# Expert stage of a two-layer hybrid decoder step: one unrolled stream over both expert tables instead of a u pass and a v pass per tile

## The chip, the cores and the metric

One core of one Trainium2 chip. The time is device microseconds (us) of the whole program, median of several runs. Everything is float32.

## What is computed

One inference step of a trunk of two layers (DEPTH = 2) for 512 prompt tokens and 8 decoding sequences. A layer has three token mixers, an output projection, and then the PEER feed-forward part, which the change is about. Cut to that part:

```python
def peer_ffn(h, wq, sub_keys, u_tab, v_tab):
    ...
    s = jnp.einsum('nhpk,hpek->nhpe', q, sub_keys).astype(jnp.float32)
    s1, i1 = lax.top_k(s[:, :, 0], PEER_TOPK)
    s2, i2 = lax.top_k(s[:, :, 1], PEER_TOPK)
    ...
    top_s, pick = lax.top_k(cand_s, PEER_TOPK)
    idx = jnp.take_along_axis(cand_i, pick, axis=-1).reshape(n, PEER_HEADS * PEER_TOPK)
    gate = jax.nn.softmax(top_s, axis=-1).reshape(n, PEER_HEADS * PEER_TOPK)
    ...
        act = jax.nn.gelu(jnp.einsum('nd,ned->ne', xk, u_tab[ik]).astype(jnp.float32), approximate=False)
        return jnp.einsum('ne,ned->nd', (gk * act).astype(v_tab.dtype), v_tab[ik])
```

Each token picks 8 heads x 16 = 128 experts of 16384. An expert is a row of 1024 floats in table u and one in table v. A token's output is the sum over its 128 experts of gate x gelu(u row . x) x v row.

## The kernel before

**Tiling.** The 512 prompt tokens are four tiles (t = 0 to 3) of 128 tokens, a token to a partition. One *gather* is an indirect DMA from POOL that fetches, for one of the 128 slots, one row of a table for each of the 128 tokens: 128 rows of 4 KB, 524,288 bytes, into one buffer of 128x1024. A tile needs 128 gathers from u and 128 from v; a layer 1024. The 8 decoding tokens are a fifth, small tile that comes behind them with 16 gathers (line 1614).

**Order.** The expert stage is one block in which the engines run programs of their own, tied by semaphores. POOL goes through the tiles, in each first through all of u, then all of v, in a loop over 16 slots (line 1602). For each four slots it waits for four free buffers of a ring of 16 (line 1604), copies four columns of indices to a small tile (line 1605), waits for this copy (line 1606) and issues four gathers (line 1608).

DVE takes the buffers in the same order. In the u half of a tile it multiplies a buffer by the token's activations O and sums (line 1753, `tensor_tensor_reduce`, shown as CUSTOM_DVE_ANT_0); after 128 of them ACT takes the gelu (line 1657), DVE multiplies by the gates, and in the v half DVE adds each buffer times its weight to one of two sums (line 1773, `scalar_tensor_tensor`). Both halves are loops over 16 slots, cut into four segments.

**choose(t + 1)**, the top-k work for the next tile on DVE (lines 1671 to 1742), is a generator of 15 steps; one or two of its steps stand behind each segment. Its last step lets POOL begin the next tile (`dve2pool`). The scores it starts from are eight matmuls (line 1624) and four copies on ACT (line 1644).

**Layers.** The whole layer is the body of a device loop (line 1834), so the layer number is a register, and so are the addresses and semaphore values made from it.

## Time and profile before

| | us |
|---|---|
| time, median of 3 runs | 6643.17 |
| the 3 runs | 6636.66 to 6656.37 |
| span of the profiled execution | 6651.1 |
| expert stage of layer 0, first gather to last weighted row | 1509.87 to 3278.60 |
| expert stage of layer 1 | 4817.40 to 6592.90 |

The profile is one execution, and its page gives the span, 6651.1 us, as its time. The stage just named is run twice and takes 1768.7 and 1775.5 us. A row of the profile names the line, the engine, the operation and the shapes; a number behind `|` or in brackets is the time for which the engine had nothing to do just before, with what ended it. `POOLq`, `DVEq` are the engine's own sequencer (its waits, branches and registers).

### The profile page before, as it was taken

Reading aid. Unit: us, or ns where it says so; the run is one execution under the profiler, and the core shown is the slowest. Engines: PE = TensorE matmul, PEld = TensorE weight load, DVE = VectorE, ACT = ScalarE, POOL = GpSimd, SP = SyncE. Lnnn points to the kernel's source line nnn. Section 1 sums busy time; section 2 is a strip of 40 time slices with the busy share of each in tenths; the row PEclk is TensorE's granted clock in tenths of the full one; section 3 lists DMA queues with packets and bytes.
Section 4 is the critical chain, followed back from the end, with each engine's and each line's share of the span. In section 5 each row is a group of like instructions: output and inputs, shape, how many; then the busy total and the mean of one; then the engine's idle time right before and its main releaser. Section 6 shows DMA issues by size and latency. Waiting matters only on the chain. (4 is left out here: it accounts for less than half of the span.)

```text
span 6651.1 us, 37510 instructions
## 1 busy us (share of the span) xinstructions
PE 2041.9 (31%) x6954; PEld 1122.8 (17%) x6954; DVE 4002.0 (60%) x7053; ACT 442.1 (7%) x877; POOL 2699.0 (41%) x2674
## 2 busy tenths in 40 slices
PE   7966446760000000000079664467500000000000
PEld 2434125430000000000024331364300000000000
DVE  1222442247887977978812325422478889788787
ACT  1112011110000000000011120111100000000000
POOL 0000001006777777777600000020077777776775
PEclk8975667875555555555589766678755555555555
DMA  5101520007888988989751016101089889888897
GB/s 205 51 29 39 172 59 0 28 29 266 308 304 284 329 284 295 328 285 316 282 180 51 29 39 190 41 1 34 27 299 315 299 292 328 283 300 302 286 315 270
DMA packets 463974, 1292.69 MB, mean 194 GB/s; under 512 B 50768, under 2 KB 155289, under 8 KB 463590
## 3 DMA queue, kind: packets, MB, share of 16 engines
q0 software_dynamic: 299520, 1090.65, 47.5%
q1 hardware_dynamic: 127400, 166.42, 7.8%
q10 hardware_dynamic: 36864, 33.57, 1.6%
q8 instruction: 60, 0.98, 0.1%
q14 instruction: 130, 1.06, 0.1%
HBM read 1279.23 MB, written 11.44 MB: 194 GB/s over the span
## 5 line engine op out<-in xcount | busy, mean ns | idle before, releaser
L1753 DVE CUSTOM_DVE_ANT_0 arena<-arena 128x1024 f32<-128x1024 f32 x1024 | 1229.0, 1225 | 407.4 <-DMA arena<-in_peer_u_dram,arena 380.9
L1608 POOL DMA_INDIRECT arena<-in_peer_u_dram,arena x1024 | 1277.7, 1248 | 447.8 <-issue 207.7
L1773 DVE SCALAR_TENSOR_TENSOR arena<-arena 128x1024 f32<-128x1024 f32 x1024 | 1256.6, 1289 | 83.4 <-DMA arena<-in_peer_v_dram,arena 66.4
L1608 POOL DMA_INDIRECT arena<-in_peer_v_dram,arena x1024 | 1072.1, 1047 | 449.4 <-POOLq L1606 207.4
L1624 PE MATMUL bank<-arena 128*128 128x256 f32 (+1 forms) x160 | 49.4, 476 | 1995.7 <-PEq L1622 1993.1
L1630 PE MATMUL bank<-arena 8*128 8x512 f32 x8 | 7.5, 1087 | 1638.9 <-PEq L1628 1638.9
L907 POOL TENSOR_TENSOR arena<-arena 128x512 f32<-128x512 f32 x56 | 70.7, 1265 | 1039.1 <-SPq L898 794.0
L1210 POOL MEMSET arena<- 128x2048 f32 (+1 forms) x4 | 5.5, 1382 | 944.4 <-POOLq L693 944.4
L1624 PEld LDWEIGHTS bank<-arena 128*128 128x128 f32 (+1 forms) x160 | 33.8, 217 | 2010.5 <-issue 2003.3
L1605 POOL COPY arena<-arena 128x4 int32 x512 | 227.2, 444 | 343.0 <-POOLq L1604 339.9
L440 PE MATMUL bank<-arena 128*128 128x512 f32 (+5 forms) x896 | 323.3, 518 | 0.0
L1630 PEld LDWEIGHTS bank<-arena 8*128 8x128 f32 x8 | 2.3, 319 | 1641.9 <-issue 1641.9
L943 DVE TENSOR_TENSOR arena<-arena,bank 128x512 f32<-128x512 f32 x56 | 38.5, 688 | 261.3 <-DVEq L941 261.3
L264 PE MATMUL bank<-arena 128*9 128x512 f32 x384 | 168.5, 602 | 36.7 <-PEq L260 36.7
L1340 PE MATMUL bank<-arena 128*4 128x256 f32 x512 | 143.4, 450 | 116.7 <-PEq L1339 116.7
L440 PEld LDWEIGHTS bank<-arena 128*128 128x128 f32 (+1 forms) x896 | 142.7, 161 | 176.8 <-issue 162.5
L436 PE MATMUL bank<-arena 128*128 128x512 f32 x384 | 171.3, 608 | 1.9 <-PEq L430 1.9
L1657 ACT ACT_TABLE_LOAD x8 | 10.3, 1283 | 2211.9 <-ACTq L1656 2211.9
L1515 POOL MEMSET arena<- 128x2048 f32 x2 | 3.6, 1804 | 368.7 <-POOLq L293 368.7
L1671 DVE MAX8 arena<-arena 128x8 f32<-128x128 f32 (+3 forms) x240 | 59.2, 320 | 154.7 <-DVEq L1695 153.1
L1394 DVE TENSOR_TENSOR arena<-arena 128x2048 f32<-128x2048 f32 x32 | 73.3, 2290 | 111.8 <-DVEq L1392 111.6
L1457 PE MATMUL bank<-arena 128*128 128x512 f32 (+1 forms) x320 | 138.0, 593 | 1.2 <-PEq L1450 1.2
(348 smaller groups left out, 4217.0 us busy)
## 6 DMA issues: line engine op xcount, KB each, us to landing
arena<-in_w_ada_dram SPq DMA_DIRECT2D x24, 2048.0 KB, 7.9
arena<-in_cache_sb_k_dram SPq DMA_DIRECT2D x256, 128.0 KB
arena<-in_cache_sb_v_dram ACTq DMA_DIRECT2D x256, 128.0 KB, 2.9
arena<-in_w_in_dram SPq DMA_DIRECT2D x12, 2048.0 KB
arena<-in_peer_u_dram,arena POOLq DMA_INDIRECT x1040, 5.7
arena<-in_peer_v_dram,arena POOLq DMA_INDIRECT x1040, 5.9
arena<-in_w_out_dram SPq DMA_DIRECT2D x2, 4096.0 KB
arena<-in_peer_wq_dram SPq DMA_DIRECT2D x2, 4096.0 KB
```

Source lines behind the costliest of these rows:

```text
L264: last = pe_.matmul(ps[n % 2][0:R9, :], CT[:, k, :], W[n % 3][:, k, :], start=(k == 0), stop=(k == KD - 1))
L436: mm = pe_.matmul(ps[i % BANKS][:, :], W[n % 2][:, k, off:off + P], HT[:, k, 0:SEQ], start=(k == 0), stop=(k == KD - 1))
L440: mm = pe_.matmul(ps[i % BANKS][0:rows, 0:hi - lo], HT[:, k, t * P:t * P + rows], W[n % 2][:, k, 0:hi - lo], start=(k == 0), stop=(k == KD ...
L907: nc.gpsimd.tensor_tensor(H4(LM[n % 2]), H4(L[:, t, :]), bc(m, 1, NH), ALU.mult).then_inc(pool2pe, 1)
L1340: last = pe_.matmul(ps[b % 2][0:NH, 0:AW], by_page(SFB, b)[:, j, :], VB[i][:, j % HP, :], start=(j == 0), stop=(j == PAGES - 1))
L1394: vec.tensor_tensor(kb, kb, bc(QB[:, b, :], 1, HP), ALU.mult).then_inc(dve_own, 1)
L1457: last = pe_.matmul(ps[2 + g % 2][0:rows, :], OT[:, k, t * P:t * P + rows], W[:, k, half * GBLK:(half + 1) * GBLK], start=(k == 0), stop=( ...
L1605: nc.gpsimd.tensor_copy(IS[lot], IDI[:, t, bass.ds(i * GR + lot * LOT, LOT)]).then_inc(pool_own, 1)
L1608: pool.indirect_dma_start(G_[lot * LOT + j], None, tables[which], bass.IndirectOffsetOnAxis(ap=IS[lot][:, j:j + 1], axis=0)).then_inc(gath ...
L1624: last = pe_.matmul(ps[h // 2][0:rows, (h % 2) * 256:(h % 2) * 256 + 256], QT[:, h, t * P:t * P + rows], KBD[:, h, :], start=True, stop=True)
L1753: vec.tensor_tensor_reduce(G_[j], G_[j], O[:, t, :], 1.0, 0.0, ALU.mult, ALU.add, A8[:, j:j + 1]).then_inc(ring_free, 1)
L1773: vec.scalar_tensor_tensor(a, G_[j], AV[:, bass.ds(i * GR + j, 1)], a, ALU.mult, ALU.add).then_inc(dve_own, 1)
```

## The change

The layer loop becomes a Python loop, so that the program holds each layer's instructions once per layer. In the expert stage all loops are unrolled, and u and v run side by side:

- The 16 buffers become two rings of eight, U_ and V_. Unit u is one slot of one tile, 512 units in a layer. At unit u POOL issues the u gather of unit u and the v gather of unit u - 20 (LAG), each straight from the index column of the tile IDI, with a wait for the buffer that was used eight units ago. The index copies and their waits are gone.
- DVE takes the dot product of unit u. ACT takes the gelu for lots of 16 units, DVE multiplies a lot by the gates.
- Of four v rows, three go to PE: ACT makes a diagonal matrix from the weight column (`DG`, ring of four), and two matmuls of 128x512 add diagonal x rows to banks 6 and 7. The fourth is added on DVE as before. At a tile's end DVE adds the two banks to its own sum.
- One of the 15 steps of choose(t + 1) stands behind every eighth unit of tile t.

```diff
-        GR = 16
-        LOT = 4
-        gathered = [sem(f"gathered{i}") for i in range(GR)]
+        RING = 8
+        LOT = 16
+        LAG = 20
+        DIAGS = 4
+        u_landed = [sem(f"u_landed{i}") for i in range(RING)]
+        r_landed = [sem(f"r_landed{i}") for i in range(RING)]
+        u_done = sem("u_done")
+        sums_done = sem("sums_done")
+        prods_done = sem("prods_done")
+        lot_gelu = sem("lot_gelu")
+        lot_gated = sem("lot_gated")
+        diag_made = sem("diag_made")
+        banks_read = sem("banks_read")
...
-            G_ = [MOD9[:, i * D:(i + 1) * D] for i in range(5)] + [AR.room(D) for _ in range(GR - 5)]
-            IS = [AR.room(LOT).bitcast(I32) for _ in range(GR // LOT)]
-            A8 = AR.room(GR)
-            AV = AR.room(SLOTS)
...
+            G_ = [MOD9[:, i * D:(i + 1) * D] for i in range(5)] + [AR.room(D) for _ in range(2 * RING - 5)]
+            U_, V_ = G_[0:RING], G_[RING:2 * RING]
+            DG = [AR.room(P) for _ in range(DIAGS)]
+            A8 = AR.room(PH)
+            A = [AR.room(SLOTS) for _ in range(2)]
+            AV = [AR.room(SLOTS) for _ in range(2)]
...
-            ACC = [AR.room(D) for _ in range(2)]
-            JK = ACC[1]
+            ACC = AR.room(D)
...
+            by_pe = lambda v: v % 4 != 3
+            n_pe = lambda v: sum(by_pe(i) for i in range(v))
+            n_dve = lambda v: v - n_pe(v)
+            UNITS = NT * SLOTS
+            landed = lambda l, i: 16 * (l * (UNITS + PH) // RING + i // RING + 1)
+            CHOOSE_EVERY = 8
+            STEPS = 15
...
-                        pool.wait_ge(dve2pool, 1).then_inc(dve2pool, -1)
-                        for which in range(2):
-                            with pool.Fori(0, SLOTS // GR) as i:
-                                for lot in range(GR // LOT):
-                                    pool.wait_ge(ring_free, LOT).then_inc(ring_free, -LOT)
-                                    nc.gpsimd.tensor_copy(IS[lot], IDI[:, t, bass.ds(i * GR + lot * LOT, LOT)]).then_inc(pool_own, 1)
-                                    pool.wait_ge(pool_own, 1).then_inc(pool_own, -1)
-                                    for j in range(LOT):
-                                        pool.indirect_dma_start(G_[lot * LOT + j], None, tables[which],
-                                                                bass.IndirectOffsetOnAxis(ap=IS[lot][:, j:j + 1], axis=0)).then_inc(gathered[lot * LOT + j], 16)
+                    for u in range(UNITS + LAG):
+                        v = u - LAG
+                        if u < UNITS:
+                            if u % SLOTS == 0:
+                                pool.wait_ge(dve2pool, 1).then_inc(dve2pool, -1)
+                            if u >= RING:
+                                pool.wait_ge(u_done, l * UNITS + u - RING + 1)
+                            pool.indirect_dma_start(U_[u % RING], None, tables[0],
+                                                    bass.IndirectOffsetOnAxis(ap=IDI[:, u // SLOTS, u % SLOTS:u % SLOTS + 1], axis=0)).then_inc(u_landed[u % RING], 16)
+                        if v >= 0:
+                            if v >= RING:
+                                if by_pe(v - RING):
+                                    pool.wait_ge(prods_done, l * n_pe(UNITS) + n_pe(v - RING + 1))
+                                else:
+                                    pool.wait_ge(sums_done, l * n_dve(UNITS) + n_dve(v - RING + 1))
+                            pool.indirect_dma_start(V_[v % RING], None, tables[1],
+                                                    bass.IndirectOffsetOnAxis(ap=IDI[:, v // SLOTS, v % SLOTS:v % SLOTS + 1], axis=0)).then_inc(r_landed[v % RING], 16)
...
+                    scores(0)
+                    for u in range(UNITS + LAG):
+                        if u % SLOTS == 0 and u < UNITS:
+                            scores(u // SLOTS + 1)
+                        v = u - LAG
+                        if v < 0 or not by_pe(v):
+                            continue
+                        n = n_pe(v)
+                        first, last_ = n_pe(v - v % SLOTS) == n, n_pe(v - v % SLOTS + SLOTS) == n + 1
+                        if first and v >= SLOTS:
+                            pe.wait_ge(banks_read, l * NT + v // SLOTS)
+                        pe.wait_ge(diag_made, l * n_pe(UNITS) + n + 1)
+                        pe.wait_ge(r_landed[v % RING], landed(l, v))
+                        for i in range(2):
+                            mm = pe_.matmul(ps[6 + i][:, :], DG[n % DIAGS], V_[v % RING][:, i * GBLK:(i + 1) * GBLK],
+                                            start=first, stop=last_, skip_group_check=True)
+                        mm.then_inc(prods_done, 1)
...
-                    for t in range(NT):
-                        scores(t + 1)
-                        act.wait_ge(dve2act, 1).then_inc(dve2act, -1)
-                        act_.activation(AV, AV, ACT.Gelu).then_inc(act2dve, 1)
-                        gate_exp(t + 1)
+                    made = 0
+                    for u in range(UNITS + LAG):
+                        t, s_ = u // SLOTS, u % SLOTS
+                        if s_ == 0 and u < UNITS:
+                            scores(t + 1)
+                        if s_ == (STEPS - 2) * CHOOSE_EVERY + 1 and u < UNITS:
+                            gate_exp(t + 1)
+                        if u % LOT == 0 and 0 < u <= UNITS:
+                            lo = u - LOT
+                            a = A[lo // SLOTS % 2][:, lo % SLOTS:lo % SLOTS + LOT]
+                            act.wait_ge(u_done, l * UNITS + u)
+                            act_.activation(a, a, ACT.Gelu).then_inc(lot_gelu, 1)
+                        v = u - LAG + 2
+                        if 0 <= v < UNITS and by_pe(v):
+                            act.wait_ge(lot_gated, (l * UNITS + v) // LOT + 1)
+                            if made >= DIAGS:
+                                act.wait_ge(prods_done, l * n_pe(UNITS) + made - DIAGS + 1)
+                            act_.mul(DG[made % DIAGS], ident, AV[v // SLOTS % 2][:, v % SLOTS:v % SLOTS + 1]).then_inc(diag_made, 1)
+                            made += 1
...
-                        vec.tensor_scalar(IDX[r, t, :], IDX[r, t, :], LB[r, 0:1], None, ALU.add).then_inc(dve_own, 1)
+                        vec.tensor_scalar(IDX[r, t, :], IDX[r, t, :], float(l * EXPERTS), None, ALU.add).then_inc(dve_own, 1)
...
-                    for t in range(NT):
-                        nxt = choose(t + 1)
...
-                            with dve.Fori(seg * PER, (seg + 1) * PER) as i:
-                                for j in range(GR):
-                                    dve.wait_ge(gathered[j], l * per_layer[j] + (i * 16 + (done + 16)))
-                                    vec.tensor_tensor_reduce(G_[j], G_[j], O[:, t, :], 1.0, 0.0, ALU.mult, ALU.add, A8[:, j:j + 1]).then_inc(ring_free, 1)
-                                vec.engine_nop().then_inc(dve_own, 1)
-                                vec.wait_ge(dve_own, 1).then_inc(dve_own, -1)
-                                vec.tensor_copy(AV[:, bass.ds(i * GR, GR)], A8).then_inc(dve_own, 1)
...
-                        done += SLOTS // GR * 16
-                        dve.sem_inc(dve2act, 1)
-                        dve.wait_ge(act2dve, 1).then_inc(act2dve, -1)
...
-                        for seg in range(SEGS):
-                            dve.sem_inc(dve_own, 1)
...
-                                for j in range(GR):
-                                    dve.wait_ge(gathered[j], l * per_layer[j] + (i * 16 + (done + 16)))
-                                    a = ACC[j % 2]
-                                    vec.scalar_tensor_tensor(a, G_[j], AV[:, bass.ds(i * GR + j, 1)], a, ALU.mult, ALU.add).then_inc(dve_own, 1)
-                                    dve.wait_ge(dve_own, 1).then_inc(dve_own, -1)
-                                    dve.sem_inc(ring_free, 1)
-                            dve.wait_ge(dve_own, 1).then_inc(dve_own, -1)
-                            next(nxt, None)
...
+                    summed = 0
+                    for u in range(UNITS + LAG + 1):
+                        t, s_ = u // SLOTS, u % SLOTS
+                        if u < UNITS:
+                            dve.wait_ge(u_landed[u % RING], landed(l, u))
+                            vec.tensor_tensor_reduce(U_[u % RING], U_[u % RING], O[:, t, :], 1.0, 0.0, ALU.mult, ALU.add,
+                                                     A[t % 2][:, s_:s_ + 1]).then_inc(u_done, 1)
+                            if s_ == 0:
+                                nxt = choose(t + 1)
+                            if s_ % CHOOSE_EVERY == 0:
+                                next(nxt, None)
+                            assert s_ < SLOTS - 1 or next(nxt, "over") == "over"
+                        if u % LOT == 1 and LOT < u <= UNITS + 1:
+                            lo = u - 1 - LOT
+                            w, c = lo // SLOTS, slice(lo % SLOTS, lo % SLOTS + LOT)
+                            dve.wait_ge(lot_gelu, (l * UNITS + u - 1) // LOT)
+                            vec.tensor_tensor(AV[w % 2][:, c], A[w % 2][:, c], GT[:, w, c], ALU.mult).then_inc(lot_gated, 1)
+                        v = u - LAG
+                        if 0 <= v < UNITS and not by_pe(v):
+                            g = AV[v // SLOTS % 2][:, v % SLOTS:v % SLOTS + 1]
+                            dve.wait_ge(lot_gated, (l * UNITS + v) // LOT + 1)
+                            dve.wait_ge(r_landed[v % RING], landed(l, v))
+                            if n_dve(v - v % SLOTS) == summed:
+                                vec.tensor_scalar(ACC, V_[v % RING], g, None, ALU.mult).then_inc(sums_done, 1)
+                            else:
+                                dve.wait_ge(sums_done, l * n_dve(UNITS) + summed)
+                                vec.scalar_tensor_tensor(ACC, V_[v % RING], g, ACC, ALU.mult, ALU.add).then_inc(sums_done, 1)
+                            summed += 1
+                        if v > 0 and v % SLOTS == 0:
+                            w = v // SLOTS - 1
+                            dve.wait_ge(prods_done, l * n_pe(UNITS) + n_pe(v))
+                            dve.wait_ge(sums_done, l * n_dve(UNITS) + n_dve(v))
+                            for i in range(2):
+                                c = slice(i * GBLK, (i + 1) * GBLK)
+                                mm = vec.tensor_tensor(ACC[:, c], ACC[:, c], ps[6 + i][:, :], ALU.add)
+                            mm.then_inc(banks_read, 1)
+                            dve.wait_ge(banks_read, l * NT + w + 1)
+                            vec.tensor_tensor(ACC, ACC, GP, ALU.mult).then_inc(dve_own, 1)
+                            vec.wait_ge(dve_own, 1).then_inc(dve_own, -1)
+                            vec.tensor_tensor(X[:, w, :], X[:, w, :], ACC, ALU.add).then_inc(dve_own, 1)
+                            vec.wait_ge(dve_own, 1).then_inc(dve_own, -1)
...
-        with nc.Fori(0, DEPTH) as l:
+        for l in range(DEPTH):
```

The order in which POOL issues, in the expert stage: before, four gathers of one table behind each index copy, and the other table only in another loop.

```order
L1605 ISA [waits ring_free]
L1605 COPY arena<-arena 128x4
L1608 DMA arena<-in_peer_u_dram,arena 128x1024 [waits pool_own]
L1608 DMA arena<-in_peer_u_dram,arena 128x1024 x3
L1602 REGISTER_ALU
L1602 COMPARE_AND_BRANCH
L1602 UNCONDITIONAL_BRANCH
```

With the change, at the same place (POOL, from the unit at which the v ring has gone round once):

```order
L1621 DMA arena<-in_peer_u_dram,arena 128x1024 [waits u_done]
L1629 DMA arena<-in_peer_v_dram,arena 128x1024 [waits prods_done]
L1621 DMA arena<-in_peer_u_dram,arena 128x1024 [waits u_done]
L1629 DMA arena<-in_peer_v_dram,arena 128x1024 [waits prods_done]
L1621 DMA arena<-in_peer_u_dram,arena 128x1024 [waits u_done]
L1629 DMA arena<-in_peer_v_dram,arena 128x1024 [waits sums_done]
```

Copy, its wait and the loop are gone, and each gather now carries a wait of its own: for a dot product on DVE (`u_done`), for products on PE (`prods_done`) or for a sum on DVE (`sums_done`).

DVE before, where a u loop ends (the dot products of line 1753 appear as ISA, each with a second row that reads its sum):

```order
L1753 ISA arena<-arena 128x1024 [waits gathered15]
L1753 ISA arena 128x1
L1754 ISA
L1756 ISA [waits dve_own]
L1756 COPY arena<-arena 128x16
L1750 REGISTER_ALU [waits dve_own]
L1750 COMPARE_AND_BRANCH
```

DVE with the change, around a step of choose (lines 1777 and 1781) and a lot's gates (line 1820):

```order
L1830 SCALAR_TENSOR_TENSOR arena<-arena 128x1024 [waits sums_done,r_landed3,lot_gated]
L1809 ISA arena<-arena 128x1024 [waits u_landed0]
L1809 ISA arena 128x1
L1777 TENSOR_TENSOR arena<-arena 128x2048
L1781 TENSOR_TENSOR arena<-arena 128x256 [waits dve_own]
L1781 TENSOR_TENSOR arena<-arena 128x256 x7
L1809 ISA arena<-arena 128x1024 [waits dve_own,u_landed1]
L1809 ISA arena 128x1
L1820 TENSOR_TENSOR arena<-arena 128x16 [waits lot_gelu]
L1809 ISA arena<-arena 128x1024 [waits u_landed2]
```

The weighted rows now stand among the dot products, one to four units, and the steps of choose one by one between them.

## Rows read from the trace of the kernel before

**Rows 1.** The page: span, and busy tenths in 40 slices.

```profile
span 6651.1 us, 37510 instructions
...
POOL 0000001006777777777600000020077777776775
...
DMA  5101520007888988989751016101089889888897
```

**Rows 2.** Groups: line, engine, op, shapes | busy, mean | idle before; 1506 to 3310.

```profile
L1608 POOL DMA_INDIRECT arena<-in_peer_u_dram,arena x512 | 639.9, 1250 | 224.0 <-issue 104.9 <-POOLq L1606 103.8 <-POOLq L1604 14.6
L1773 DVE SCALAR_TENSOR_TENSOR arena<-arena 128x1024 f32<-128x1024 f32 x512 | 628.2, 1289 | 37.6 <-DMA arena<-in_peer_v_dram,arena 29.0 <-DVEq L1768 7.5
L1753 DVE CUSTOM_DVE_ANT_0 arena<-arena 128x1024 f32<-128x1024 f32 x512 | 614.5, 1225 | 204.6 <-DMA arena<-in_peer_u_dram,arena 191.4 <-DVEq L1757 4.1 <-DVEq L1678 2.2
L1608 POOL DMA_INDIRECT arena<-in_peer_v_dram,arena x512 | 533.2, 1041 | 224.2 <-POOLq L1606 103.7 <-issue 97.0 <-POOLq L1604 22.6
L1605 POOL COPY arena<-arena 128x4 int32 x256 | 112.8, 441 | 171.1 <-POOLq L1604 169.5
```

**Rows 3.** Groups on POOL in the u half of tile 0 (1509 to 1744).

```profile
L1608 POOL DMA_INDIRECT arena<-in_peer_u_dram,arena x128 | 161.1, 1258 | 56.8 <-issue 26.7 <-POOLq L1606 26.1 <-POOLq L1604 3.7
L1605 POOL COPY arena<-arena 128x4 int32 x32 | 15.6, 486 | 1.1 <-POOLq L1604 0.9
```

**Rows 4.** Groups on POOL in the v half of tile 0 (1744 to 1953).

```profile
L1608 POOL DMA_INDIRECT arena<-in_peer_v_dram,arena x128 | 134.1, 1048 | 55.3 <-POOLq L1606 26.0 <-issue 23.8 <-POOLq L1604 5.2
L1605 POOL COPY arena<-arena 128x4 int32 x32 | 12.5, 392 | 8.2 <-POOLq L1604 8.0
```

**Rows 5.** Timeline, u half: start us, us, engine, line, work, idle before it.

```profile
1558.37 1.23 DVE L1753 CUSTOM_DVE_ANT_0 arena<-arena 128x1024 f32<-128x1024 f32 x1 [0.67 <-DMA arena<-in_peer_u_dram,arena]
1558.54 1.89 POOL L1608 DMA_INDIRECT arena<-in_peer_u_dram,arena  x1 [0.81 <-POOLq L1606]
...
1560.55 1.22 DVE L1753 CUSTOM_DVE_ANT_0 arena<-arena 128x1024 f32<-128x1024 f32 x1 [0.94 <-DMA arena<-in_peer_u_dram,arena]
1560.73 1.85 POOL L1608 DMA_INDIRECT arena<-in_peer_u_dram,arena  x1 [0.30 <-issue]
```

**Rows 6.** Timeline of POOL in a v half.

```profile
1779.59 0.36 POOL L1605 COPY arena<-arena 128x4 int32 x1
1780.77 1.17 POOL L1608 DMA_INDIRECT arena<-in_peer_v_dram,arena  x1 [0.82 <-POOLq L1606]
```

**Rows 7.** Windows: us, busy us of each engine, PEclk, DMA share, GB/s.

```profile
1509.87:3278.60 1768.73, 17.60 (x48) 11.18 (x48) 1489.34 (x2514) 18.50 (x28) 1285.72 (x1279) 0.50 0.88 304
...
1509.00:1744.00 235.00, 6.62 (x16) 4.99 (x16) 177.13 (x403) 0.00 (x0) 176.62 (x160) 0.51 0.85 283
1744.00:1953.00 209.00, 0.00 (x0) 0.00 (x0) 193.37 (x226) 5.12 (x8) 146.07 (x160) 0.50 0.91 324
1770.00:1780.00 10.00, 0.00 (x0) 0.00 (x0) 10.00 (x10) 0.00 (x0) 7.51 (x9) 0.50 0.99 358
```

**Rows 8.** Line 1608 alone in layer 1 (4700 to 6651): durations, first and last start.

```profile
L1608 POOL DMA_INDIRECT arena<-in_peer_u_dram,arena x512: 933/1060/1993, 4817.4 to 6383.0; - x171
L1608 POOL DMA_INDIRECT arena<-in_peer_v_dram,arena x512: 933/938/2417, 5045.9 to 6585.8; - x171
...
DMA to landing us min/median/max: 4.2/5.8/6.9
```

**Rows 9.** Groups with shapes on PE and ACT, same stretch as rows 2.

```profile
L1630 PE MATMUL bank<-arena 8*128 8x512 f32 x4 | 3.7, 1085 | 812.6 <-PEq L1628 812.6
L1624 PEld LDWEIGHTS bank<-arena 128*128 128x128 f32 x32 | 9.5, 303 | 561.3 <-issue 559.1
L1650 ACT ACTIVATE arena<-arena 128x128 f32<-128x128 f32 x4 | 1.2, 309 | 58.2 <-ACTq L1649 58.2
```

**Rows 10.** Timeline of DVE where layer 1's last tile ends.

```profile
6590.35 2.53 DVE L1773 SCALAR_TENSOR_TENSOR arena<-arena 128x1024 f32<-128x1024 f32 x2 [0.57 <-DMA arena<-in_peer_v_dram,arena]
```

57 lines of the change are left out of this document (18 added, 39 removed).

## The prediction

> **What bounds the kernel now.** I read the page first. Its 40 slices show two equal layers; in each the second half is the expert stage, the stretch in which POOL is busy and the DMA engines stand at eight and nine tenths [rows 1]. The stage takes 1768.7 us in layer 0 [rows 7]. Layer 1's gathers start 1768.4 us apart, first to last (6585.8 - 4817.4) [rows 8]; over 1023 intervals that is 1.729 us a gather. The rest of the program keeps its instructions, so everything hangs on this number.
>
> Three resources could set it. DVE is busy 1489.3 of 1768.7 us, 84%, but in the u half only 177 of 235 us [rows 7], and its dot products wait 191 us a layer for rows to land [rows 2]: DVE is not first. The DMA engines show a share of 0.85 in the u half and 0.91 in the v half [rows 7]: not full. POOL has little busy time by the page, but adding the idle time in front of its instructions shows that it hardly ever waits for anybody: in the u half 161.1 + 56.8 + 15.6 + 1.1 = 234.6 of 235 us, of which the wait for free buffers at line 1604 is 0.9 [rows 3]. In the v half the sum is 210, with 8.0 us of waiting for the next tile's indices [rows 4]. Over the layer, durations and gaps of gathers and copies without that before the copies are 639.9 + 224.0 + 533.2 + 224.2 + 112.8 = 1734.1 us [rows 2], 98% of the stage. **POOL's issuing is the bound.**
>
> Why a gather costs POOL what it does: its shortest duration is 0.933 us and the median in v is 0.938 [rows 8], but the mean in u is 1.250 [rows 2]. The timeline tells why [rows 5]: a gather that starts inside a dot product ends 0.83 us after this dot product ends (1558.37 + 1.23 = 1559.60, end at 1560.43), the next one the same (1561.77, end at 1562.58, 0.81 later). The issue stands still until the dot product is over.
>
> The Trainium skill (SBUF — State Buffer, section "Who interferes with whom") says that a DVE instruction with two SBUF inputs and a GpSimd instruction that reads SBUF exclude each other for a whole instruction. For line 1753 the trace agrees with it. By this rule line 1773, which also reads two, would hold the issue up too; the v half has a median of 0.938 under it [rows 8], so the measurement decides against. If the rule held in full, the 128 weighted rows that stay on DVE would add about 0.4 us each, 50 us a layer.
>
> **The change part by part.**
>
> *Index copies and their waits, removed.* Copies: 112.8 us over 1024 gathers, 0.110 each. The gap in front of a gather is 448.2 / 1024 = 0.438 on average [rows 2] and 0.30 where no own wait stands [rows 5]; that is another 0.138. Real waits of POOL are 1768.7 - 1734.1 = 34.6 us, 0.034 each; those at a tile's end go, since choose(t + 1) ends 15 units before POOL needs its indices. 1.729 - 0.282 = 1.447 us. Check: mean duration 1173.1 / 1024 = 1.146, plus 0.30, is 1.446. The first gather behind a copy takes 1.17 us even in the v half [rows 6], 0.23 over the median; should that go with the copy, it is up to 0.06 a gather more, which I don't count. The new waits are on semaphores that were passed long before (below), so I leave the gap at 0.30; at the worst each would cost the 0.5 us by which 0.81 stands over 0.30, which would show as 1.95 a gather, but line 1604's own waits come with 0.30 in front of a gather, and I take that.
>
> *Dot products spread out.* They number 512 as before, but stand among 1024 gathers instead of 512. In the u half one held an issue up by 1.250 - 0.938 = 0.312 us, with issues 1.83 us apart (235 / 128). With issues 1.5 apart a dot product meets more of them: 0.312 x 1.83 / 1.5 = 0.38. That is 0.07 x 512 = 36 us a layer, 0.035 a gather. POOL then needs **1.48**. Bounds: no more meetings than now, 1.447; every unit loses a whole dot product of 1.225, the slower case below.
>
> *DMA.* At 1.48 the DMA engines must move 524,288 bytes each 1.48 us, 354 GB/s. The best ten microseconds in the stage show 358 GB/s at a share of 0.99 [rows 7], 1.464 us a gather; the v half's 324 at 0.91 comes to 356 at full share. So the two are level, and neither waits wholly for the other. With the share at 0.97 the DMA side gives 1.464 / 0.97 = **1.51**, and that is my value: 0.03 over either alone. The u half's 283 at 0.85 gives 333 at full share, 1.574; that end stays in the range.
>
> *Three of four v rows from DVE to PE.* This takes 0.75 x 628.2 = 471 us from DVE, leaving 1018 of about 1545, 66%. DVE was not the bound, so this gives nothing by itself; it lets u and v share the time. On PE the nearest row is a 512-column matmul at a granted clock of 0.50 [rows 7], the 1.2 GHz level, 1.085 us, with a weight load of at most 0.303 in front [rows 9]: 2 x 1.39 = 2.8 us a row, 2.1 us a unit against 2 x 1.51 = 3.02. PE stays hidden. ACT's diagonal is at most 0.309 [rows 9], three in four units, hidden as well, the gelu and its table load too.
>
> *Two rings of eight.* A buffer is asked for again after eight units, 24 us. A u row needs 5.8 us to land [rows 8] and 1.3 for the dot product, so DVE may stand still for some 17 us. Its longest pause is the first step of choose, where PE's scores queue behind two or three products (some 8 us), ACT copies them and DVE does 16 maxima: about 14 us by these. Hidden, barely. If that cover is short by 5 us, it costs 5 x 4 tiles x 2 layers = 40 us. A v row needs 5.8 + 2.8 and the gates of its lot, which are made three units before POOL gets to it.
>
> *Unrolled layer loop, unrolled stage.* Static addresses spare some register work on queues that wait anyway: 0 to 5 us. The longer program must be fetched, between other DMAs; the stretches without loops run today at the same pace, so I take 0.
>
> *Ends.* The last row still lands, is added on DVE (1.3 us) [rows 10] and goes through three or four adds. No change.
>
> **Sum.** 1023 x 1.51 = 1544.7 us instead of 1768.4: 223.7 us less a layer, 447 in all. The profiled span of 6651.1 is 8 us over the median and inside the three runs, so the saving can be taken from the median: 6643.2 - 447.4 = **6196 us**.
>
> **The rivals.** Each is a pace; the time is 6643.2 - 2 x (1768.4 - 1023 x pace).
>
> 1. *DMA is the bound at the u half's rate.* For it: reads from two tables, irregular rows, 333 GB/s at full share in the u half. Against: in that half POOL left gaps, and a share with gaps says little. 1.574 gives 6327.
> 2. *POOL is the bound and DMA doesn't matter.* For it: 358 GB/s is only what POOL let through. Against: the share was 0.99 there. 1.447 gives 6067. The Trainium skill (DMA: Bandwidth & Descriptors, section "Measured") has 425 GB/s for large loads on one core, which by its figure would be an estimated 1.23 us a gather and would leave POOL alone at 1.48, 6135; its section "Where 436 GB/s comes from" names some 358 for HBM, as the trace does.
> 3. *Slower: POOL falls in step with the dot products.* Each unit has two issues and one dot product. If DVE starts each just ahead of an issue, as in [rows 5], a unit costs 2 x 1.24 + 1.225 = 3.705 us, 1.853 a gather: 1895.6 us a layer, **6898**. It decides from 2 x 1.729 - 2.48 = 0.98 us lost per dot product; the u half shows 0.31, which speaks against it.
> 4. *The rings run dry or the code comes late.* A pause of POOL between units, 0.1 to 0.2 a gather: 1.61 to 1.70, 6400 to 6585.
> 5. *The change does not do what it says*: the tile's last products and the bank reads tie the v stream to the tile's end, and DMA pauses there as now (8 us of waiting at a tile's end [rows 4]). Three times a layer, 48 us in all: 6244, inside my range.
>
> **How the numbers follow.** My case, 1.48 to 1.54 (6135 to 6257): 0.42; rival 5 beside it: 0.05. Rival 1, 1.54 to 1.61 (to 6400): 0.22. Rival 2 and faster, under 1.48: 0.20. Rival 4: 0.07. Rival 3 or another that ends slower: 0.03; within 0.3% of no change, which is about what a measurement of this kernel can tell: 0.01. Range 6080 to 6390: it leaves out the outer part of rival 2, and rivals 3 and 4. Faster by over 0.3%: 0.96 by these cases.
>
> **What would show it.** Gathers of one layer, first to last, 1545 us; POOL with no copies, gaps of 0.30, mean duration near 1.2; DMA share 0.95 and over in the whole stage, at 345 to 350 GB/s; DVE at 66% with its idle time in front of dot products, released by DMA; PE busy under 70% there. Wrong if POOL waits for `prods_done` or `u_done` (rings), if the mean duration of a gather is over 1.3 (contention), or if landing takes far over 6 us while POOL waits (DMA bound at a lower rate).

## The result, and the profile after

The changed kernel takes 6003.53 us (median of 4 runs, 5986.12 to 6017.0), the kernel before, on the same chip, 6639.91 us (4 runs, 6629.24 to 6656.37). The ratio is 0.903, with a 95% interval of 0.900 to 0.906. The saving is 636 us, where 447 were predicted, and 6004 lies below the whole range (6080 to 6390).

The page of the changed kernel: its span, busy times, and POOL, DMA and GB/s in 40 slices, to be held against [rows 1].

```profile
span 6013.3 us, 38811 instructions
...
PE 3855.7 (64%) x10026; PEld 1787.5 (30%) x10026; DVE 3037.1 (51%) x6267; ACT 739.0 (12%) x1699; POOL 2414.6 (40%) x2162
...
POOL 0000000100777777777600000001017777777775
...
DMA  6110350010999999999851004400119999999998
GB/s 227 49 39 0 119 165 14 1 57 5 346 370 385 364 380 373 363 376 362 313 198 56 32 0 148 136 14 1 62 51 351 366 381 356 366 372 369 376 358 301
```

The stage's DMA digits, eights and nines before, are nines. From its first gather's start to its last gather's start, the stage of layer 0 went from 1761.7 to 1445.7 us and that of layer 1 from 1768.4 to 1466.9: 316.0 and 301.5 us of the 637.8 by which the two spans differ. The other 20 lie outside.

Inside, the gathers of layer 0 run from 1507.9 to 2953.6. POOL's two groups (line, engine, op, shapes, count | busy us, mean ns | idle before, with releasers) and then POOL's waits over 1500 to 3000 us:

```profile
L1629 POOL DMA_INDIRECT arena<-in_peer_v_dram,arena x512 | 580.4, 1134 | 156.1 <-issue 138.1 <-PE bank L1667 18.0
L1621 POOL DMA_INDIRECT arena<-in_peer_u_dram,arena x512 | 554.3, 1083 | 297.4 <-issue 155.8 <-POOLq L1618 141.6
```

```profile
POOL arena L1621 <- issue: 155.8, 511, 0.3
POOL arena L1621 <- POOLq L1618: 141.6, 1, 141.6
POOL arena L1629 <- issue: 138.1, 453, 0.3
POOL arena L1629 <- PE bank L1667: 18.0, 59, 0.3
```

The 141.6 us stand before the first gather of the stage. The rest adds up: 580.4 + 554.3 + 155.8 + 156.1 = 1446.6 us, and the stage's 1023 intervals take 1445.7. No gap is longer than 0.31 us. POOL waits for nobody, not even where the releaser is named PE. Against [rows 2] the copies are gone, the gaps fell from 0.438 to 0.305 a gather, and the gathers' mean went from 1.146 to 1.108. The pace, the time from one gather's start to the next one's, is 1.413 us in layer 0 and 1.434 in layer 1. I had forecast 1.51.

DVE's and PE's main groups in the same stretch, and the windows of the whole stage and of its first full part (us, busy us of PE, PEld, DVE, ACT and POOL, PEclk, DMA share, GB/s):

```profile
L1809 DVE CUSTOM_DVE_ANT_0 arena<-arena 128x1024 f32<-128x1024 f32 x512 | 623.3, 1226 | 385.6 <-DMA arena<-in_peer_u_dram,arena 374.4 <-DVEq L1731 1.5 <-DVEq L1746 1.5
L1830 DVE SCALAR_TENSOR_TENSOR arena<-arena 128x1024 f32<-128x1024 f32 x124 | 159.3, 1284 | 39.9 <-DMA arena<-in_peer_v_dram,arena 20.7 <-issue 11.6
```

```profile
L1667 PE MATMUL bank<-arena 128*128 128x512 f32 x1536 | 912.8, 743 | 588.5 <-DMA arena<-in_peer_v_dram,arena 554.7 <-ACT arena L1715 20.5 <-DVE arena L1838 13.0
```

```profile
1507.90:2953.60 1445.70, 913.94 (x1564) 338.88 (x1565) 1006.00 (x2122) 168.06 (x439) 1133.77 (x1023) 0.83 0.98 370
1540.00:1700.00 160.00, 100.25 (x168) 36.34 (x168) 118.93 (x295) 17.92 (x49) 124.62 (x117) 0.82 1.00 380
```

DVE is busy 1006 of 1446 us (70%) and waits for rows; PE is busy 914 (63%) and waits for rows. The core's transfers reach 380 GB/s at a share of 1.00, where [rows 7] had 358 at 0.99.

What is left to explain is the gathers' length. Seven entries of POOL and DVE in the timeline of the changed kernel, others between them left out (start us, us, engine, line, work):

```profile
2066.54 0.94 POOL L1621 DMA_INDIRECT arena<-in_peer_u_dram,arena  x1 [0.30 <-issue]
...
2067.02 1.23 DVE L1809 CUSTOM_DVE_ANT_0 arena<-arena 128x1024 f32<-128x1024 f32 x1 [1.59 <-DMA arena<-in_peer_u_dram,arena]
...
2067.78 1.28 POOL L1629 DMA_INDIRECT arena<-in_peer_v_dram,arena  x1 [0.30 <-issue]
...
2068.34 1.28 DVE L1830 SCALAR_TENSOR_TENSOR arena<-arena 128x1024 f32<-128x1024 f32 x1
...
2069.36 1.07 POOL L1621 DMA_INDIRECT arena<-in_peer_u_dram,arena  x1 [0.30 <-issue]
...
2070.70 2.29 DVE L1777 TENSOR_TENSOR arena<-arena 128x2048 f32<-128x2048 f32 x1
2070.74 3.06 POOL L1629 DMA_INDIRECT arena<-in_peer_v_dram,arena  x1 [0.30 <-issue]
```

Each long gather ends 0.81 us after the DVE instruction inside which it began: 2067.78 + 1.28 = 2069.06 against 2067.02 + 1.23 = 2068.25; 2069.36 + 1.07 = 2070.43 against 2069.62; 2070.74 + 3.06 = 2073.80 against 2072.99. These are a dot product (line 1809), a weighted sum (line 1830) and a step of choose (line 1777); each reads two operands from SBUF. I then held one formula against all records of gathers that begin at least 0.1 us into such an instruction: duration = the larger of 0.938 and (end of the DVE instruction + 0.81 - start). It meets 443 of the 444 measured durations under dot products of layer 0 within 0.05 us, and all 117 under weighted sums. What a gather takes over 0.938 us is called its excess; it is the cost that the experiments look for.

The same trace has a control: a reduction of line 1785 is as long as the step of choose above, but reads one tensor.

```profile
2144.43 2.28 DVE L1785 TENSOR_REDUCE arena<-arena 128x128 f32<-128x2048 f32 x1
...
2145.62 0.93 POOL L1621 DMA_INDIRECT arena<-in_peer_u_dram,arena  x1 [0.30 <-issue]
```

In this trace 16 gathers, and in that of the kernel before 26, begin at least 0.1 us inside such a reduction with no other DVE instruction under way: none is held up, where the formula would give up to 2.5 us.

### The profile page after: what moved, and what is told of

Its sections match the earlier page's. It is cut to its first block and busy times, and to the rows that moved or that the text cites. A ratio compares the mean times of both kernels' runs of the same rounds, so it can differ in the third digit from the quotient of the medians.

```text
span 6013.3 us, 38811 instructions
## 1 busy us (share of the span) xinstructions
PE 3855.7 (64%) x10026; PEld 1787.5 (30%) x10026; DVE 3037.1 (51%) x6267; ACT 739.0 (12%) x1699; POOL 2414.6 (40%) x2162
## 5 line engine op out<-in xcount | busy, mean ns | idle before, releaser
L1667 PE MATMUL bank<-arena 128*128 128x512 f32 x3072 | 1829.8, 744 | 1192.4 <-DMA arena<-in_peer_v_dram,arena 1128.6
L1809 DVE CUSTOM_DVE_ANT_0 arena<-arena 128x1024 f32<-128x1024 f32 x1024 | 1246.4, 1225 | 788.1 <-DMA arena<-in_peer_u_dram,arena 766.2
L1667 PEld LDWEIGHTS bank<-arena 128*128 128x128 f32 x3072 | 672.1, 235 | 2346.2 <-issue 2041.5
L1621 POOL DMA_INDIRECT arena<-in_peer_u_dram,arena x1024 | 1120.0, 1094 | 594.7 <-issue 311.6
L1629 POOL DMA_INDIRECT arena<-in_peer_v_dram,arena x1024 | 1170.5, 1143 | 312.3 <-issue 277.8
L1715 ACT ACTIVATE arena<-arena 128x128 f32<-128x128 f32 x768 | 294.5, 398 | 2136.9 <-PE bank L1667 1683.9
L1830 DVE SCALAR_TENSOR_TENSOR arena<-arena 128x1024 f32<-128x1024 f32 x248 | 318.6, 1285 | 85.6 <-DMA arena<-in_peer_v_dram,arena 41.3
L450 PEld LDWEIGHTS bank<-arena 128*128 128x128 f32 (+1 forms) x896 | 142.7, 161 | 176.9 <-issue 162.5
L446 PE MATMUL bank<-arena 128*128 128x512 f32 x384 | 170.8, 606 | 2.1 <-PEq L440 2.1
L928 PE MATMUL bank<-arena 128*128 128x128 f32 x448 | 78.2, 330 | 121.8 <-PEq L926 100.1
L937 PE MATMUL bank<-arena 128*128 128x128 f32 x448 | 118.4, 358 | 0.0
L938 PE MATMUL bank<-arena 128*128 128x128 f32 x448 | 116.5, 354 | 0.0
```

What stands on the lines that cost most here:

```text
L446: mm = pe_.matmul(ps[i % BANKS][:, :], W[n % 2][:, k, off:off + P], HT[:, k, 0:SEQ], start=(k == 0), stop=(k == KD - 1))
L450: mm = pe_.matmul(ps[i % BANKS][0:rows, 0:hi - lo], HT[:, k, t * P:t * P + rows], W[n % 2][:, k, 0:hi - lo], start=(k == 0), stop=(k == KD ...
L937: pe_.matmul(ps[2 + n % 2][:, hs(h)], T[:, t, hs(h)], YB[n % 2][:, hs(h)], start=True, stop=True)
L1621: pool.indirect_dma_start(U_[u % RING], None, tables[0], bass.IndirectOffsetOnAxis(ap=IDI[:, u // SLOTS, u % SLOTS:u % SLOTS + 1], axis=0) ...
L1629: pool.indirect_dma_start(V_[v % RING], None, tables[1], bass.IndirectOffsetOnAxis(ap=IDI[:, v // SLOTS, v % SLOTS:v % SLOTS + 1], axis=0) ...
L1667: mm = pe_.matmul(ps[6 + i][:, :], DG[n % DIAGS], V_[v % RING][:, i * GBLK:(i + 1) * GBLK], start=first, stop=last_, skip_group_check=True)
```

## The experiments

**Theory.** POOL's issue is the bound before and after; a gather costs 0.305 of gap and 0.938 of its own, and the rest is the time for which DVE's instructions hold it up. **Rivals:** the transfers set the pace (at 358 GB/s or more); the rings; the layer loop; the pace comes from removing copies alone.

All are the kernels named, timed in rounds with the kernel before on the same chip, whose median was 6656.8 for the first four, 6634.9 for the next four, 6653.1 for e9 to e11 and 6654.0 for e12. The changed kernel stood in none of these rounds, so differences against its 6003.5 are uncertain by up to some 20 us, by which the medians of the kernel before differ.

This table is worked out from the records of the gathers in layer 0 (layer 1 in brackets where it differs by over 0.01): 1024 gathers, 1023 intervals, us. A gap here is all the time between two gathers, index copies included. The last two columns are the sums of the excess of gathers that began inside a dot product, and inside a weighted sum.

```
kernel               us    pace           duration  gap     in dots  in sums
before            6639.9   1.722          1.146     0.576   162      41
after             6003.5   1.413 (1.434)  1.108     0.305   138      22
e1_no_dots        5745.7   1.294          0.986     0.308     0      39
e2_stt_dots       6010.7   1.435          1.130     0.305   150      26
e3_layers         6651.2   1.725 (1.740)  1.143     0.582   158      41
e4_direct         6406.2   1.601          1.120     0.481   179       5
e5_copies         6547.2   1.680          1.155     0.524   184      18
e6_one_of_four    6109.1   1.473          1.168     0.305   166      60
e7_four_deep      6114.9   1.472 (1.483)  1.127     0.345   152      25
e8_psum_operand   5767.1   1.308          1.000     0.308     1      50
e9_half_dots      5828.0   1.339 (1.325)  1.034     0.305    27      54
e10_all_on_pe     5772.0   1.299          0.950     0.349     0       0
e11_before_psum   6324.7   1.557          0.990     0.567     2      40
e12_half_rows     5729.2   1.277          0.966     0.311     4       0
```

**e1: dot products of one column** (the other 1023 are left out), on the changed kernel:

```
- vec.tensor_tensor_reduce(U_[u % RING], U_[u % RING], O[:, t, :], 1.0, 0.0, ALU.mult, ALU.add,
-                          A[t % 2][:, s_:s_ + 1]).then_inc(u_done, 1)
+ vec.tensor_tensor(A[t % 2][:, s_:s_ + 1], U_[u % RING][:, 0:1], O[:, t, 0:1], ALU.mult).then_inc(u_done, 1)
```

> The changed kernel, with each dot product over 1024 columns replaced by a product of one column; the dot products are left out, all gathers, weighted sums and waits stay. POOL theory (issuing a gather is the bound, and what is over 0.94 + 0.30 us of it is mostly blocking by the dot products): the pace falls from 1.42 to 1.26 to 1.30 us a gather, total 5710 to 5790 us, POOL still without waits. DMA theory (the engines are full at a share of 0.98, POOL's fullness is a coincidence): the pace stops at 1.37 to 1.40, total 5900 to 5960, a gather takes far more than 6.2 us to land and POOL waits for free buffers.

Measured: 5745.73 us (5740.25 to 5748.93), ratio 0.863. The window of the stage that I read:

```profile
1700.00:2000.00 300.00, 206.81 (x364) 79.97 (x364) 102.46 (x362) 39.62 (x101) 229.23 (x233) 0.85 1.02 406
```

406 GB/s: the transfers set no bound at 358, nor at 380. The work on DVE alone made 258 us, though DVE was not the bound. One sign of the DMA theory did come: rows take longer to land, where the changed kernel has 6.2 and 6.3 us, though POOL still waits for nobody (gaps 0.308).

```profile
arena<-in_peer_u_dram,arena POOLq DMA_INDIRECT x1040, 8.6
arena<-in_peer_v_dram,arena POOLq DMA_INDIRECT x1040, 8.9
```

**e2: the same dot products by another instruction.**

```
- vec.tensor_tensor_reduce(U_[u % RING], U_[u % RING], O[:, t, :], 1.0, 0.0, ALU.mult, ALU.add, A[...])
+ vec.scalar_tensor_tensor(U_[u % RING], U_[u % RING], 1.0, O[:, t, :], ALU.mult, ALU.mult, accum_out=A[...])
```

> The changed kernel, with the dot product computed by scalar_tensor_tensor with an accumulated output (U x 1.0 x O, summed) instead of tensor_tensor_reduce. The weighted sums of the kernel before, the same kind of instruction, left issues at their shortest. POOL theory, and this form doesn't block: as without dot products, 5710 to 5790 us, gathers' mean duration under 1.0. If this form blocks as the other does: 5990 to 6020. DMA theory: 5900 to 5960 with landings over 7 us.

Measured: 6010.7 us (6003.43 to 6025.34), as the changed kernel, with about the same excess (150 and 149 us in the two layers for 138 and 153). It is not the custom instruction: scalar_tensor_tensor holds gathers up in the same way.

**e3: the layer loop alone**, on the kernel before (`with nc.Fori(0, DEPTH) as l:` becomes `for l in range(DEPTH):`).

> The kernel before, with only the device loop over the two layers replaced by a Python loop. Of the 638 us by which the spans differ, some 18 lie outside the two expert stages. Theory: they come from static addresses and from the missing loop end: 6610 to 6630 us. Rival: they come from the work left warm or early by the new expert stage: 6635 to 6645.

Measured: 6651.23 us, ratio 0.9985 (0.997 to 1.0001): 0 to 20 us, most likely 5 to 10, and none of it in the stage (pace 1.725). Neither expected range was met; they stood on 6640 for the kernel before, which took 6656.8 in these rounds, and moved up by those 17 us the rival's is 6652 to 6662. The part that I had put at 0 to 5 is small indeed; of the 20 us outside the stages at most this much is explained, and the rest stays open.

**e4: direct index columns and no copies, halves kept**, on the kernel before:

```
- with pool.Fori(0, SLOTS // GR) as i:
+ for i in range(SLOTS // GR):
...
-         nc.gpsimd.tensor_copy(IS[lot], IDI[:, t, bass.ds(i * GR + lot * LOT, LOT)]).then_inc(pool_own, 1)
-         pool.wait_ge(pool_own, 1).then_inc(pool_own, -1)
...
-                                 bass.IndirectOffsetOnAxis(ap=IS[lot][:, j:j + 1], axis=0))
+                                 bass.IndirectOffsetOnAxis(ap=IDI[:, t, at:at + 1], axis=0))
```

> The kernel before, with POOL's loop unrolled and the index column given to each gather directly, without index copies and their waits; u pass and v pass, one ring of 16 and all of DVE's work stay. POOL theory: copies and own waits cost 0.25 us a gather, but DVE with 84% of the stage is next at about 1.48 a gather: pace 1.50 to 1.53, total 6190 to 6240 us. Rival (most of the gain is from u and v side by side, the copies are cheap or covered): pace over 1.60, total over 6380.

Measured: 6406.15 us (6386.34 to 6414.23), ratio 0.962: 250 us, not 400 or more. Windows of its first u half and v half, DVE's weighted rows and POOL's waits in the v half:

```profile
1508.80:1722.20 213.40, 5.21 (x16) 4.04 (x16) 174.53 (x399) 0.00 (x0) 169.58 (x128) 0.52 0.89 308
1722.20:1928.20 206.00, 0.00 (x0) 0.00 (x0) 196.37 (x230) 5.12 (x8) 122.14 (x129) 0.50 0.86 333
```

```profile
L1772 DVE SCALAR_TENSOR_TENSOR arena<-arena 128x1024 f32<-128x1024 f32 x128 | 158.2, 1311 | 2.0 <-DVEq L1767 1.9
```

```profile
POOL arena L1607 <- issue: 34.2, 112, 0.3
POOL arena L1607 <- POOLq L1604: 30.6, 4, 9.8
```

In the u half POOL is still the bound: 169.6 us of gathers and 43.8 of gaps are the 213.4. In the v half it no longer is. Gathers take 0.954 us there and would need 128 x 1.26 = 161 us; but the half takes 206, of which DVE is busy 196, and POOL waits up to 9.8 us for free buffers. So the copies hid that DVE was just behind. In the gather records such waits (gaps over 0.305) come to 45 us in this half and to 316 us over the 8 v halves, and to 41 over the u halves. They go when u and v stand side by side with rows moved off DVE: 250 + 316 + 41 = 607 of the 636 measured. The two parts of the change are worth much less apart than together; e5 prices the other one.

**e5: copies put back**, on the changed kernel:

```
+ if u % 4 == 0:
+     nc.gpsimd.tensor_copy(IS[0][u // 4 % 4], IDI[:, u // SLOTS, u % SLOTS:u % SLOTS + 4]).then_inc(pool_own, 1)
+     pool.wait_ge(pool_own, 1).then_inc(pool_own, -1)
...
-                         bass.IndirectOffsetOnAxis(ap=IDI[:, u // SLOTS, u % SLOTS:u % SLOTS + 1], axis=0))
+                         bass.IndirectOffsetOnAxis(ap=IS[0][u // 4 % 4][:, u % 4:u % 4 + 1], axis=0))
```

and the same for v.

> The changed kernel with index copies put back: before every fourth gather of each table GpSimd copies four index columns to a buffer of its own and waits for that copy. If GpSimd's own instruction stream sets the pace of the two rings (theory), each gather gets longer by the share of a copy and of the wait: in the kernel before that was 0.22 to 0.28 us a gather, which over 2046 gathers gives 450 to 570 us, so 6450 to 6570. If the transfers or the ring set the pace (rival), GpSimd's time is covered: 6000 to 6060.

Measured: 6547.2 us (6542.43 to 6551.96). POOL's groups in layer 0:

```profile
L1636 POOL DMA_INDIRECT arena<-in_peer_v_dram,arena x512 | 596.4, 1165 | 226.5 <-issue 122.9 <-POOLq L1635 101.2 <-PE bank L1674 2.1
L1625 POOL DMA_INDIRECT arena<-in_peer_u_dram,arena x512 | 586.6, 1146 | 221.1 <-issue 117.9 <-POOLq L1624 103.0 <-DVE arena L1816 0.3
L1634 POOL COPY arena<-arena 128x4 int32<-128x4 int32 x128 | 52.3, 409 | 0.0
L1623 POOL COPY arena<-arena 128x4 int32<-128x4 int32 x128 | 37.2, 290 | 141.6 <-POOLq L1619 141.1
```

6547.2 - 6003.5 = 544 us over 2046 intervals is 0.266 a gather; the prediction had 0.282 for this step. In layer 0 that is 0.219 in the gaps, copies included, and 0.047 in longer gathers, since more of them meet dot products early (excess 184 us for 138). POOL sets the pace on both sides of the change. Against the kernel before, this kernel, which has all of the change but the direct index columns, gains 88 us (ratio 0.985, 0.981 to 0.989): apart the two parts give 250 and 88, together 636.

**e6: one of four weighted rows on PE, three on DVE** (`by_pe = lambda v: v % 4 == 0`).

> The changed kernel with the shares swapped: one of four weighted rows on TensorE, three of four on VectorE (384 sums a layer there and not 128). VectorE's work in the stream rises by 256 x 1.285 = 329 us a layer, to about 1260 of 1446 us. Theory (GpSimd's issue is the bound, VectorE's work costs only by the gathers that it makes longer): sums made the gathers under them longer by 0.19 us each, 117 of 128 sums had such a gather, so about 256 x 0.19 = 49 us a layer, 6060 to 6150. Rival (VectorE becomes the bound, its rings run dry): above 6250.

Measured: 6109.12 us (6107.62 to 6113.26). The window from 1600 to 2700 us:

```profile
1600.00:2700.00 1100.00, 358.11 (x424) 118.30 (x424) 965.52 (x1748) 49.21 (x137) 871.31 (x751) 0.58 0.97 358
```

DVE is busy 966 of 1100 us, 88%, and POOL's gap is still 0.305: DVE is no bound. The 106 us come from longer gathers: 38 us more in weighted sums and 28 in dot products in layer 0, 26 and 17 in layer 1.

**e7: rings of four** (each gather waits for the unit four back, and not eight).

```
- pool.wait_ge(u_done, l * UNITS + u - RING + 1)
+ pool.wait_ge(u_done, l * UNITS + u - 4 + 1)
```

and the same for v.

> The changed kernel with only four rows of each table in flight and not eight (each gather waits for the row four units back). A row takes 6.2 us to land and a unit takes 2.85 us, and then the row must be used: four units are 11.4 us, about 6.2 + 2.9 + 1.3 = 10.4 us are needed. Theory: the rings of eight have room, with four the pace is kept in most places and lost where VectorE does other work: 6020 to 6150. Rival (the rings of eight were barely enough, as the prediction had it): above 6250.

Measured: 6114.86 us (6092.1 to 6135.56): with four, 111 us are lost. POOL's waits in the same 1100 us:

```profile
POOL arena L1621 <- issue: 113.4, 372, 0.3
POOL arena L1629 <- issue: 102.3, 326, 1.8
POOL arena L1629 <- PE bank L1667: 18.9, 55, 0.9
POOL arena L1621 <- DVE arena L1809: 13.3, 9, 2.3
```

Waits up to 2.3 us come in. Some 80 of the 111 us are in the gaps (0.345 and 0.343 for 0.305), the rest in longer gathers. Eight buffers are not barely enough; four would almost do.

**e8: the dot products' second operand in PSUM**, on the changed kernel. Banks 4 and 5, which are free during the stream, become one tensor `OB` of 1024 columns:

```
+ if s_ == 0:
+     if u:
+         dve.wait_ge(u_done, l * UNITS + u)
+     vec.tensor_copy(OB[:, :], O[:, t, :]).then_inc(dve_own, 1)
+     vec.wait_ge(dve_own, 1).then_inc(dve_own, -1)
...
- vec.tensor_tensor_reduce(U_[u % RING], U_[u % RING], O[:, t, :], 1.0, ...
+ vec.tensor_tensor_reduce(U_[u % RING], U_[u % RING], OB[:, :], 1.0, ...
```

> The changed kernel with the second operand of the dot products in PSUM: VectorE copies the tile of 1024 columns to two free banks once for each tile of 128 rows, and all 512 dot products of a layer read one operand from SBUF and one from PSUM. Theory: GpSimd's gathers are made longer by what VectorE reads from SBUF with two operands at once; then the 133 to 150 us a layer of that in the dot products go, and the time is 5715 to 5790. Rival (a dot product makes a gather longer by writing and reading SBUF at all, whatever its second operand): 6000 to 6030. A second rival, that GpSimd's gathers wait for the transfers' queues at more than 380 GB/s: 5850 to 5960.

Measured: 5767.09 us (5764.05 to 5777.03), ratio 0.868 (0.8645 to 0.8714). Against the changed kernel that is another 236 us. Its timeline:

```profile
2064.16 0.93 POOL L1632 DMA_INDIRECT arena<-in_peer_v_dram,arena  x1 [0.31 <-issue]
...
2064.45 1.22 DVE L1817 CUSTOM_DVE_ANT_0 arena<-arena,bank 128x1024 f32<-128x1024 f32 x1 [1.33 <-DMA arena<-in_peer_u_dram,arena]
2065.40 0.94 POOL L1624 DMA_INDIRECT arena<-in_peer_u_dram,arena  x1 [0.30 <-issue]
...
2065.78 1.28 DVE L1838 SCALAR_TENSOR_TENSOR arena<-arena 128x1024 f32<-128x1024 f32 x1
...
2066.64 1.23 POOL L1632 DMA_INDIRECT arena<-in_peer_v_dram,arena  x1 [0.30 <-issue]
```

The gather at 2065.40 begins 0.95 us into a dot product and takes 0.94; with both operands in SBUF it would have ended 0.81 after it, 1.08. The one at 2066.64 begins inside a weighted sum, which still reads two from SBUF, and ends 0.81 after it (2067.87 against 2067.06). Of the 454 gathers that begin inside a dot product of layer 0 with no other DVE work started, three took 1.15 us and all others under 1.0: the excess is 1 us where it was 138. DVE does exactly the same work in the same time (1.219 us a dot product), rows and transfers are the same. The excess in dot products is 290 us less over both layers, that in weighted sums 48 more (their phases moved): 242 by this sum, 236 measured. This is the cause, shown by itself.

**e9: half of each dot product** (512 of 1024 columns; the other half is left out).

> The changed kernel with dot products over the first 512 of the 1024 columns (the other half of each dot product is left out): a dose between the changed kernel (1024 columns, 6003 us) and the version with one column (5746 us). Theory: what a dot product costs is the time for which it makes GpSimd's gathers longer, and that goes with how long it reads two operands from SBUF: half of the 133 to 150 us a layer goes, so 5860 to 5890. Rival (it costs once at its start or end, however long it is): 5980 or more. Rival (it costs nothing once it is shorter than a gather, 0.94 us): 5750 to 5780.

Measured: 5828.03 us (5821.36 to 5833.76), below the 5860 to 5890 of my theory in the form that I gave it. A dot product of 0.692 us costs 27 us a layer and not half of 138. The formula says why it is less than half: a gather that begins p us into an instruction of length D (its phase) loses D - p - 0.13 us, so summed over phases that are spread evenly the loss goes with (D - 0.13) squared: (0.692 - 0.13)² / (1.226 - 0.13)² = 0.26, and 0.26 x 138 = 36. Measured are 27 and 19; so the phases are not spread evenly, and that part is not explained. Part of the gain goes again: the excess in weighted sums is 54 and 48 us, where it was 22 and 28.

**e10: e8 with all weighted rows on PE** (`by_pe = lambda v: True`; the banks are copied to `ACC` and not added).

> The version with the dot products' second operand in PSUM (5767 us), and with all four of four weighted rows on TensorE, none on VectorE. The 128 sums of a layer made gathers longer by about 0.43 us each for 112 of them: 48 us in a layer. Theory (GpSimd's issue is still the bound at 404 GB/s): 2 x 45 us go, 5665 to 5700. Rival 1 (TensorE, whose product takes 2.28 us where a unit would take 2.5 us, comes too late and the v ring runs dry at times): 5730 to 5850. Rival 2 (the transfers have a bound near 405 GB/s): 5750 to 5780.

Measured: 5771.98 us (5767.1 to 5776.09), the same as e8. The excess is gone (gathers 0.950), but gaps have come in. POOL's groups in layer 0, the window, and how long a row takes from issue to landing:

```profile
L1624 POOL DMA_INDIRECT arena<-in_peer_u_dram,arena x512 | 490.7, 958 | 321.3 <-POOLq L1621 141.7 <-issue 136.1 <-DVE arena L1816 43.5
L1632 POOL DMA_INDIRECT arena<-in_peer_v_dram,arena x512 | 482.1, 942 | 177.5 <-issue 127.5 <-PE bank L1669 50.0
```

```profile
1600.00:2700.00 1100.00, 837.99 (x1749) 296.92 (x1748) 711.23 (x1659) 183.61 (x473) 812.38 (x855) 1.00 1.02 408
```

```profile
arena<-in_peer_u_dram,arena POOLq DMA_INDIRECT x1040, 14.8
arena<-in_peer_v_dram,arena POOLq DMA_INDIRECT x1040, 14.9
```

In e8 rows landed after 6.6 us, here after 14.8 to 14.9, and POOL's idle time before gathers is put down to dot products (43.5 us) and to products (50.0), which wait for rows. In these numbers is the 0.3 us of each gap; what stands over it is 45 us a layer. The rival of PE can be told apart: PE is busy 838 of 1100 us here and 859 in e12, where the long gaps are gone. Transfers queue: rival 2, a bound near 408 GB/s.

**e12: e10 with rows of 2 KB**, as many gathers, half of the bytes (the other half of each row is left out). A view of the tables with rows of 512 columns takes their place, and 16 memsets, 7.5 us in all, stand ahead of each layer's gathers.

> The version with all weighted rows on TensorE, and each of the 2048 gathers of a layer's stream brings rows of 2 KB into the first 512 columns of its buffer and not rows of 4 KB (the other half of each row, and with it half of what is computed from it, is left out; the second halves are set to zero once before the stream, by 16 memsets that cost 5 to 12 us a layer). As many gathers, as many rows, half of the bytes. In the version before it GpSimd's gathers took 0.955 us and gaps of over 0.31 us had come in, rows took 14.8 us to land and the cores moved 408 GB/s. Theory (there the bytes became the bound, no longer GpSimd): the pace goes from 1.322 to 1.24 to 1.27 us a gather, the landing time falls below 6 us, and the time is 5640 to 5700. Rival (it is the number of rows or the users of the rows that set 1.32 us): 5770 to 5800, with the landing time as before.

Measured: 5729.23 us (5724.5 to 5736.44), 43 us less, or 58 without the memsets, and not 70 to 130. Landing time and window:

```profile
arena<-in_peer_u_dram,arena POOLq DMA_INDIRECT x1040, 3.7
```

```profile
1600.00:2700.00 1100.00, 858.53 (x1781) 305.74 (x1780) 723.90 (x1674) 187.30 (x481) 836.47 (x866) 0.99 0.72 207
```

The landing time falls to 3.7 us, the gaps to 0.311, and the pace from 1.299 to 1.277 and 1.270. So the bytes were what made POOL wait in e10, as the theory had it, but there was less to gain: gathers of half rows take 0.946 at the median and not 0.937, and steps of choose and the like lengthen them by 19 to 22 us a layer, not 14 to 16. In e10 the two bounds, POOL's issue and the bytes, are level.

**e11: the kernel before with e8's edit alone.**

> The kernel before, with one edit alone: the tile of the dot products' second operand is copied to two free PSUM banks once for each of the 4 tiles, and the dot products read it there. Theory: the 160 us a layer by which dot products made gathers longer in the u halves go (gathers there took 1.25 us and should take about 0.95 to 1.0), so 2 x 150 us: 6330 to 6370. Rival 1 (VectorE becomes late in the u halves instead, it has 1.31 us for a dot product and its read, and group ends): 6400 to 6500. Rival 2 (only the new order of the rings makes such a gain visible): above 6600.

Measured: 6324.65 us (6316.86 to 6328.24), ratio 0.951 (0.948 to 0.9545). One copy a tile gives the old kernel 328 us, just over the 283 to 323 that the expected range stood for, and half of what the whole new schedule gave: the excess of 162 and 158 us in the two layers, and a little more. The index copies gained too, from 441 ns [rows 2] to a mean of 300.

## Why the prediction was wrong, step by step

- **"POOL's issuing is the bound": right**, before and after (e5, e6, and the sum above: gathers and gaps make 1446.6 us, and the stage takes 1445.7).
- **"Index copies and their waits, removed", -0.282 a gather: right.** e5 gives 0.266. The gap is 0.305 as forecast. The 0.06 that I left out for the first gather behind a copy was no cost of the copy: outside DVE's instructions 46 such gathers of layer 0 had 1.1 us of excess together. That the whole step works out needs the halves merged, as e4 shows; the prediction gave DVE's move to PE "nothing by itself", but with the merge it gives 88 us alone (e5), and beside the direct columns it freed some 316 us of waits in the v halves.
- **"Dot products spread out", +0.035 a gather: the first step that failed.** It scaled 0.312 a dot product by how close issues stand, 0.38. Measured are 138 us in 512 dot products, 0.270 (0.300 in layer 1), and the median gather of the u stream fell to 0.940. What was wrong is the model: the loss depends on the phase. In [rows 5] two gathers start 0.17 and 0.18 us into the dot product, nearly the worst phase. Over layer 0 of the kernel before, 106 of 375 gathers that began inside a dot product did so at 1.0 us or later; in the new stream it is half of them (242 of 465 from 1540 to 2900 us), and these lose nothing or little. So POOL came to 1.413 and 1.434, mean 1.424, where I had 1.48: 0.056 x 2046 = 115 us of the 189 by which I was wrong. By the records the dot products are 0.048 of this 0.056. Another 0.018 is a gain that the prediction put at nothing: three of four weighted sums left DVE, and the excess in sums fell from 40 and 46 us a layer to 22 and 28. Slightly longer gaps and steps of choose took 0.01 back.
- **"DMA", 358 GB/s at a share of 0.99 as a cap, and 1.51 from both: the second step that failed.** The share was near 1 at 358, at 380 and at 406 GB/s alike, since it counts the time of packets, and those got shorter: a 4 KB packet took 180 ns on average in the ten microseconds of [rows 7], 170 in the changed kernel (1540 to 1700 us) and 164 in e1. Rows landed later from 406 GB/s on (8.6 us in e1), and POOL waited for them only at 408 (14.8 us in e10). With no DMA term the sum ends at POOL's own pace: 0.03 x 2046 = 61 us of the error. The other 13 of the 189 are the 20 us outside the stages, less 7 since layer 0's stage before took 1761.7 us and not layer 1's 1768.4.
- **Weighted sums cost gathers nothing: wrong.** The prediction let the v half decide against a rule. The records of e6 and after show that the sums hold gathers up by the same formula as dot products, 22 to 28 us a layer for 128 sums, 54 to 60 for 384. The v half before showed a median of 0.938 only by its phase: of 398 gathers of layer 0 that began inside a weighted sum, 229 did so in its first 0.1 us, and not one of these was held up; the other 169 follow the formula within 0.05 us. The records of the kernel before show how:

```profile
1809.02 7.35 DVE L1773 SCALAR_TENSOR_TENSOR arena<-arena 128x1024 f32<-128x1024 f32 x6
...
1811.15 1.17 POOL L1608 DMA_INDIRECT arena<-in_peer_v_dram,arena  x1 [0.81 <-POOLq L1606]
1812.63 0.94 POOL L1608 DMA_INDIRECT arena<-in_peer_v_dram,arena  x1 [0.31 <-issue]
```

  Sums in a row start every 1.225 us (7.35 / 6), and a gather with its gap takes 1.243, so they ran in step. The first gather behind a copy began 0.93 us into a sum (median) and was held up, 25 of the 40 us of excess in sums; the next three began at 0.02 to 0.06. The Trainium skill (SBUF — State Buffer, section "Who interferes with whom") was right in its rule that two SBUF inputs on DVE and a GpSimd instruction that reads SBUF contend, and in that one input outside SBUF frees GpSimd, which e8 shows with its 236 us. But that the two "exclude each other" shows in one direction only: in the changed kernel 864 dot products that began inside a gather took 1.224 us on average, the other 160 took 1.231. The 50 us a layer that the prediction worked out for that rule were 22 to 28, since sums too have harmless phases.
- **PE hidden: right, but by luck in its size.** The prediction took one record of 1.085 us for a matmul of 512 columns. But the row of line 1630 in [rows 9] has four records for two matmuls, 3.7 us busy: a weighted row, also two such matmuls and four records, costs 3.7 us at the granted clock of 0.50 and not 2.8. e6 has it, at a mean granted clock of 0.58 (1600 to 2700 us):

```profile
L1667 PE MATMUL bank<-arena 128*128 128x512 f32 x376 | 347.2, 1078 | 743.7 <-DMA arena<-in_peer_v_dram,arena 712.8 <-DVE arena L1838 30.8
```

  347.2 us for 94 rows are 3.69 each. Three rows in four units at 3.7 would be 2.8 us a unit, of the 2.85 that a unit takes. What gave room was the granted clock, which rose to 0.83 with the products on PE: 912.8 / 384 = 2.38 us a row.
- **DVE 66%:** 70%. **Rings "barely" enough:** too careful; e7. **Layer loop:** 0 to 20 us for 0 to 5; e3.
- **Rival 2** (POOL alone, 1.447, 6067) was nearest, and had 0.20. The argument against it, the share of 0.99, was worth nothing. Its own 1.447 was 0.023 too slow.

What is left: 20 us outside the stages, of which e3 explains 5 to 10 by its median; why gathers land in harmless phases, which I tell from the records and have not set by experiment; and how the 316 us of waits in the v halves divide between the merge of the halves and the move of rows to PE, since neither was run without the other. Moving back two of the four rows alone costs 106 us (e6).

## What to carry to other kernels

Where GpSimd issues indirect DMAs, read its gathers' durations against what VectorE runs at that moment: if the long ones end a fixed time after a VectorE instruction with two operands in SBUF, put one operand in PSUM before restructuring anything (here 328 us on the old kernel for one copy a tile). Price two edits that free different engines together, and look at which engine ends each half first: apart they gave 250 and 88, together 636. A DMA share near 1.00 is no bound by itself; take one only where the landing time grows and the engine that issues begins to wait for buffers. Count the records of a matmul before its mean is used as a price.

## What the hardware showed that was not expected

- A gather that begins at least 0.1 us into a VectorE instruction with two SBUF operands ends 0.81 us after it or takes its own 0.938 us, whichever is later, within 0.05 us, whatever the instruction (tensor_tensor of 2048 columns; the custom dot product; scalar_tensor_tensor). A tensor_reduce of 2.28 us, one tensor read, holds none up (0 of 16 in after, 0 of 26 in before); a tensor_scalar of 1024 columns, line 1827, one tensor and a column, does (3 of 3 in after). One that begins in the first 0.1 us slips through under a weighted sum (290 of 290 in layer 0 of before, after and e6), but mostly not under a dot product (26 of 89 in both layers of after did). Why is open.
- 4 KB rows gathered by index moved at 408 GB/s on one core; the median time from a gather's issue to its landing was 5.7 us at 302 (before), 6.6 at 402 (e8), 8.6 at 406 (e1) and 14.8 at 408 GB/s (e10).
- TensorE's granted clock over 1600 to 2700 us was 0.87 in e8 and 1.00 (the 2.4 GHz level throughout) in e10, which gave it the fourth row of four; the products of a weighted row went from 2.28 to 1.95 us, and were 3.69 in e6 at 0.58. More work made each piece cheaper.
